# Down pair 1 in both layers of a two-layer decoder trunk: seven products for a second group of four hid tiles

## What is computed

```python
h = h + mixed @ w_out
f = rms_norm(h, ffn_norm)
gate, up = jnp.split(f @ w_gate_up, 2, axis=-1)
return h + (jax.nn.silu(gate) * up) @ w_down
```

## Time and profile before

| | us |
|---|---|
| median of three runs | 1243.98 (1243.87 to 1244.28) |
| the profiled execution | 1243.3 |
| its span in the profile | 1241.4 |
| PE busy | 1229.8 (99%) |
| DVE busy | 1023.0 (82%) |
| ACT busy | 698.5 (56%) |
| POOL busy | 195.8 (16%) |

### The profile page before, as it was taken

The page is one execution under the profiler, slowest core; times in us unless marked ns, Lnnn a source line. Parts: engine busy times, 40 slices in busy tenths (PEclk is TensorE's granted clock), DMA queues, the critical chain, the costliest instruction groups (busy, mean ns, idle before and its releaser), DMA issues.

```text
span 1241.4 us, 23858 instructions
## 1 busy us (share of the span) xinstructions
PE 1229.8 (99%) x9336; PEld 1180.9 (95%) x9336; DVE 1023.0 (82%) x1692; ACT 698.5 (56%) x1158; POOL 195.8 (16%) x264
## 2 busy tenths in 40 slices
PE   7999999999999999999999999999999999999999
PEld 7999999999999999999998999888899999998998
DVE  5788888588999999897656799894899999989765
ACT  6675647655555555753345764495565555558332
POOL 3564313100000000000025663230000000000000
PEclk9999999999999999999999999999999999999999
DMA  5232111132322221233323222100323322212333
GB/s 199 87 105 71 52 35 35 35 136 83 122 103 103 102 102 69 85 99 114 111 89 104 91 73 82 35 35 18 135 103 110 129 103 103 102 69 85 119 119 119
DMA packets 27388, 114.02 MB, mean 92 GB/s; under 512 B 3472, under 2 KB 4112, under 8 KB 21904
## 3 DMA queue, kind: packets, MB, share of 16 engines
q1 hardware_dynamic: 26560, 111.45, 26.4%
q10 hardware_dynamic: 720, 1.09, 0.2%
HBM read 108.79 MB, written 2.10 MB: 89 GB/s over the span
## 4 chain that ended last, share of the span: by engine, by line
PE 97%; DVE 1%; DMA 1%; ACT 0%; issue 0%; SPq 0%; DVEq 0%; ACTq 0%
PE ps L1407 22%; PE ps L1413 11%; PE ps L1022 11%; PE ps L1118 7%; PE ps L1124 7%; PE ps L1119 7%; PE ps L1028 5%; PE ps L1491 5%; PE ps L1527 4%; PE ps L1248 3%; PE ps L1496 2%; PE ps L1532 2%; PE ps L1196 2%; PE ps L1221 2%; PE ps L1231 1%; PE ps L1305 1%
## 5 line engine op out<-in xcount | busy, mean ns | idle before, releaser
L1118 PE MATMUL ps<-xhi,whi 128*128 128x264 f32 (+1 forms) x616 | 172.0, 308 | 0.0
L1119 PE MATMUL ps<-xlo,whi 128*128 128x264 f32 (+1 forms) x616 | 167.3, 300 | 0.0
L891 POOL TENSOR_TENSOR wlo<-raw,whi 128x256 fp32r<-128x256 f32 x192 | 144.2, 783 | 141.3 <-ACT whi L1705 140.9
L1118 PEld LDWEIGHTS ps<-xhi,whi 128*128 128x128 f32 x616 | 116.1, 188 | 4.5 <-issue 1.0
L1119 PEld LDWEIGHTS ps<-xlo,whi 128*128 128x128 f32 x616 | 116.1, 189 | 3.3
L1705 ACT ACTIVATE whi<-raw 128x1024 fp32r<-128x1024 f32 x74 | 78.0, 1054 | 59.4 <-PE ps L1028 32.1
L1124 PE MATMUL ps<-xhi,wlo 128*128 128x264 f32 (+1 forms) x616 | 98.9, 303 | 0.0
L1124 PEld LDWEIGHTS ps<-xhi,wlo 128*128 128x128 f32 x616 | 85.4, 188 | 3.9
L1407 PE MATMUL ps<-fhi,hi_a 128*128 128x264 f32 (+1 forms) x352 | 88.2, 283 | 0.0
L1407 PE MATMUL ps<-flo,hi_a 128*128 128x264 f32 (+1 forms) x352 | 88.1, 282 | 0.0
L1407 PE MATMUL ps<-flo,hi_b 128*128 128x264 f32 (+1 forms) x320 | 80.3, 283 | 0.0
(11 more groups left out here) (376 smaller groups left out, 3900.5 us busy)
## 6 DMA issues: line engine op xcount, KB each, us to landing
raw<-in_weights SPq DMA_DIRECT2D x116, 512.0 KB, 3.5
raw<-in_groups SPq DMA_DIRECT2D x42, 1024.0 KB, 4.8
out_hT<-h SPq DMA_DIRECT2D x7, 256.0 KB, 4.5
h<-in_hT SPq DMA_DIRECT2D x4, 264.0 KB, 6.2
h<-in_hT ACTq DMA_DIRECT2D x4, 264.0 KB, 5.8
cst<-in_consts SPq DMA_DIRECT2D x1, 780.5 KB, 9.2
xnb<-feat SPq DMA_DIRECT2D x10, 66.5 KB, 2.0
feat<-xnb SPq DMA_DIRECT2D x10, 66.5 KB, 2.1
```

The costliest lines, as they stand in the source:

```text
L891: ins = nc.gpsimd.tensor_tensor(wlo[:, b, of], raw[:, b, of], whi[:, b, of].bitcast(F32), ALU.subtract)
L1118: nc.tensor.matmul(o, whi[:, k % 2, n], xhi[:, n, cut], start=(n == 0), stop=False)
L1119: nc.tensor.matmul(o, whi[:, k % 2, n], xlo[:, n, cut], start=False, stop=False)
```

## The change

```diff
-DN_TWO = ((2, 3), (2, 3))
+DN_TWO = ((1, 2, 3), (1, 2, 3))
...
                         if p in DN_TWO[l]:
-                            dn_weight_sums(p)
+                            if p > 1:
+                                dn_weight_sums(p)
                             for a in range(2):
                                 dn_sums_low(p, a)
                             split_down(v + 2)
                             dn_second_weight_sums(p)
                             split_down(v + 3)
+                            if p == 1:
+                                dn_second_forms_low()
                             for a in range(2):
                                 dn_second_sums_low(p, a)
                             dn_fix(p, 1, "u")
...
                         split_down(DN_UNITS * (p + 1) + m % 2)
+                    if m == 1 and 1 in DN_TWO[l]:
+                        dn_weight_sums(1)
                     if m < 2:
                         dn_forms_low(m)
```

## The result

The changed kernel takes 1252.04 us (median of 4 runs, 1251.96 to 1252.53), the kernel before 1243.92 in the same session (4 runs, 1243.26 to 1244.28). The ratio is 1.0066, with an interval of 1.0054 to 1.0078: slower by 8.1 us. The forecast was 1251.1, in a range of 1249.3 to 1253.0.

What follows compares the result with a forecast made beforehand. PE bounds the kernel (97% of the span): matmuls times spacing, while remainders arrive in time. Waits 4.5 + 4.0 less 1.39 saved make 7.1 us slower: 1250.4 from 1243.3, plus 0.7 for the median, 1251.1; range 1249.3 to 1253.0.

Steps and rivals of the forecast that it cites:

- The saving: Pair 1, tiles computed by seven products in place of eight: 0.73 us less in layer 0, 0.66 in layer 1.
- the slow first spacing: First matmul spacing after a PE stop, 0.23 in place of 0.12; mostly absorbed by the next wait, 0 to 0.1 us.
- The dates: Six points in pair 1 where PE needs DVE results; largest lags cost 4.5 us in layer 0, 4.0 in layer 1.
- form remainders: Pair 1, first group's form remainders, wanted at 72 matmuls in layer 0: 0.6 us late in each layer.
- V and P remainder: Pair 1, first remainder of the V and P weight sums, at 80 matmuls: 1.4 us late in layer 0, 0.8 in layer 1.
- fourth unit: Pair 1, remainder of the fourth weight unit, at 100 matmuls: 3.1 us late in layer 0, 2.6 in layer 1.
- second form: Pair 1, second group's form remainder, at 108 matmuls: 4.4 us late in layer 0, 3.9 in layer 1.
- second sums: Pair 1, first remainder of the second weight sums, at 112 matmuls: 4.5 us late in layer 0, 4.0 in layer 1.
- No wait: Rival: DVE delivers in time in pair 1, only the 1.39 us saving is seen, 1242.6 us; chance 0.04.
- Part of the wait: Rival: DVE's chain starts earlier or a step is shorter, by 1 to 3 us per layer; 1245 to 1249; chance 0.06.
- The clock falls: Rival: pair 1's stops bring back the lower clock, up to 1.9 us more per layer, 1254.9 us; chance 0.06.
- the landing of the fourth unit: Pair 1, layer 0: weight load lands by 556.8 at the latest, DVE wants it at 557.69, so it costs nothing.

Runs made afterwards that it cites:

- the kernel with the second form cut: Changed kernel with the second group's form remainder in two pieces, F1 in place and the rest behind the second sums' remainders; 1249.23 us, ratio 1.0042.
- The last kernel: Against the kernel with remainders in PE's demand order: first group's F5 halved, F3 and F4 separate, layer 0's two squares' sums later; 1242.54 us, ratio 0.9990.
- both GpSimd kernels: Changed kernel with the second group's form remainder made by GpSimd, in one instruction (1256.16 us) or eight pieces (1254.79 us, one execution).
- the first GpSimd kernel: Changed kernel with the second group's form remainder made by GpSimd in one instruction; 1256.16 us, ratio 1.0097.

## Why the prediction was right

**The saving** of 1.39 us. Layer 0's part is shown: without a stop, a two-group pair 1 lasts 30.06, 0.72 less. Layer 1's part is not seen as such. The length of its pair 1 in the change, 32.93, would be 29.53 - 0.66 + 4.06, and the last lag is 3.95 (below) with 0.11 for the slow first spacing behind it, so it is in line with the sum; but the one kernel that has almost no stops there keeps only 0.06.

**The dates.** PE's lag at each point is its start, less pair 1's start and the matmuls up to there at 0.1222 (in layer 1, 24 at 0.232 and the others at 0.118). In layer 0:

| matmuls | what PE waits for | forecast lag | measured |
|---|---|---|---|
| 72 | form remainders | 0.6 | 555.62 - 554.99 = 0.63 |
| 80 | V and P remainder | 1.4 | 557.38 - 555.97 = 1.41 |
| 100 | fourth unit | 3.1 | 561.50 - 558.41 = 3.09 |
| 108 | second form | 4.4 | 563.77 - 559.39 = 4.38 |
| 112 | second sums | 4.5 | 564.38 - 559.88 = 4.50 |
| 118 | other second sums | less, no stop | no stop: 565.21 - 560.61 = 4.60, the 4.50 and the restart |

In layer 1 the first five lags are 0.60, 0.79, 2.56, 3.82 and 3.95 against 0.6, 0.8, 2.6, 3.9 and 4.0. That lags are not added, only the largest counts, is shown by the kernel with the second form cut: it takes away the two steps behind 3.1 and gains 1.4 a layer, not the 1.65 (2.35 less 0.70) of DVE time that it moved.

**What the brackets don't show.** The waits in the list sum to 6.6 less the 0.35 of pair 3, 6.25 in place of 8.5. The bracket counts from the end of the row before, 0.16 after the next matmul was due, which hides 1.1 us over the seven stops. It also leaves out the 0.1 behind each stop (eight of them) and the steps too short to be listed, such as the fifth row of the table. The distance from first matmul to first matmul is what counts.

**The rivals.** "No wait" (1242.6) did not happen here. The last kernel, where every remainder is in time, has this number (1242.54), but its pairs save only 0.8 of the 1.39. "Part of the wait" fell with the table. "The clock falls" fell too, for the profiled executions of the change: behind none of their stops, up to 1.5 us, do matmuls come 0.22 apart; in layer 0 the spacing behind 563.77 is 0.23 once and 0.12 from there on. The Trainium skill (TensorE: Matmul & The Clock Gate, A second HAM failure mode: psum-queue depth-cycling) would have frequent short idle times let the clock swing; no trace here shows it at these stops. But the rival was a real one. Behind the 1.77 us stop of both GpSimd kernels the clock did fall, and in each of the two sets of four executions of the change the slowest (1252.53 and 1252.89) has a granted clock of 0.999, where the other six have 1.000. In the kernel with layer 0 only, the one execution at 0.997 took 1251.11, 3.6 above the median. In the medians of the change this weighs little. ACT was not late in the change, as forecast, and the landing of the fourth unit cost nothing: DVE has no gap ahead of 560.50.

**What was off.** The forecast is 0.9 under the measured median. The two pairs gave 7.27 where 7.1 was forecast; 0.1 in each layer is the slow first spacing behind the last stop, which the forecast named and left out of its sum. The rest is in the step from the profiled execution to the median: the medians differ by 8.1 in one session and by 7.7 in the other, while the paired profiles differ by 8.9 and 7.3. That scatter of some 0.5 is as large as what is left.

## What to carry to other kernels

When work is moved into a stage whose engines meet at fixed points, make a table of dates: when the consumer reads each piece, and when the producer is done with it by its queue. The loss is the largest lag, not the sum of lags, and not the length of the work added. Where the producer has time enough over the whole stage, as DVE had here, the repair is its order: cut an operation that serves several dates and put each part at its own. Within one session that turned +7.7 into -1.2 us, with no work removed. And GpSimd is no free helper for VectorE on operations with two inputs in SBUF.

## What the runs showed of the hardware

- **GpSimd and VectorE exclude each other, instruction by instruction.** During a 4.72 us subtraction on POOL a 1.23 us subtraction on DVE takes 4.90; against eight short ones it takes 1.65, and DVE's 0.70 operations then take up to 1.26. The Trainium skill (SBUF — State Buffer, SBUF: two separate sides) describes this: an operation of VectorE with two inputs in SBUF and one of GpSimd that reads SBUF each hold a shared pair of ports for a whole instruction, and the other one waits. The traces agree.
- **The date at which the clock rises at the start differs between executions.** Behind the wait at the start, matmuls come 0.22 apart, the lower clock level (1.2 GHz) by their spacing (the profile's granted clock reads 1.00 there too), and then 0.12 apart. The first spacing under 0.15 comes at 10.92 and 11.44 us in two profiles of the kernel before, at 13.38 and 12.79 in two of the change, and between 10.82 and 13.11 in the nine others, though all are alike up to there. Between 10.92 and 13.38 lie 11 matmuls at 0.1 more each, 1.1 us: as much as some changes are worth. Before two profiles are compared, that date is to be read in both.
- **The clock can also fall behind a stop in mid-program.** In both GpSimd kernels a stop of 1.77 us on `flo` in layer 1 is followed, some 0.9 us on, by some 3 us with matmuls 0.21 apart in place of 0.118 at a granted clock of 0.50, which costs some 1.5 us. Behind the stop of 2.87 us the spacing of 0.22 is there at once and lasts until 548.88 (granted clock 0.53 between 547 and 549). Behind a stop of 2.16 us in layer 0 of the first GpSimd kernel it is not there, nor behind any stop of up to 1.49 us in the thirteen profiles. So the length of the stop alone does not decide it, and what does was not tested.
- **A wait that is met just in time costs PE some 0.07 us** (0.19 between two starts instead of 0.118) and shows in no list of waits. That the cause is the short notice is inferred: in layer 1 the two halves of F5 and F3 end 0.15, 0.09 and 0.15 us ahead of the matmul that waits for them, in layer 0 0.75, 0.6 and 0.55 ahead, and there the steps are absent.
